# The last layer's token mixer as one block with an order per engine, and an expert ring of eight places

## What is computed

```
proj = hn @ w_in
u_pool, m_q, m_k, m_v, m_o, m_i, m_f, a_q, a_k, a_v = split(proj)
y_pool  = pool_mixer(u_pool, pool_w, pool_scale)      # window means 2, 4, 8, 16 less the value, times a 64x64 matrix
y_mlstm = mlstm_mixer(m_q, m_k, m_v, m_o, m_i, m_f)   # conv of 5 taps and silu on q, k; chunks of 128; both directions; 4 heads of 64
y_attn  = attn_mixer(a_q, a_k, a_v)                   # 8 query heads on 2 key heads of 64, head rmsnorm, rope, softmax
x = x + concatenate([y_pool, y_mlstm, y_attn]) @ w_out
x = x + mem_cross_attn(rmsnorm(x), mem)
x = x + ec_moe(rmsnorm(x))                            # 16 experts, each takes its 32 best tokens: gate-up 1024x4096, down 2048x1024
```

## Time and profile before

| | us |
|---|---|
| median of 3 runs | 4523.65 |
| lowest, highest | 4521.7, 4831.31 |
| profiled execution, its own time | 4513.02 |
| its span, first to last instruction | 4511.1 |

### The profile page before, as it was taken

One profiled execution on the slowest core, in us unless ns is written; L12 is line 12 of the kernel. 1 busy time (PEld: TensorE's weight loads), 2 busy tenths in 40 slices (PEclk: granted clock), 3 DMA queues, 4 the chain that ended last, 5 costly groups with the idle time before them and its releaser, 6 DMA issues. The chain is left out here.

```text
span 4511.1 us, 58281 instructions
## 1 busy us (share of the span) xinstructions
PE 3640.2 (81%) x19637; PEld 2637.3 (58%) x19637; DVE 2232.9 (49%) x4378; ACT 1565.4 (35%) x2639; POOL 168.1 (4%) x344
## 2 busy tenths in 40 slices
PE   7958987958699999998885599998367767767776
PEld 5638965547588888886555589997236322222223
DVE  5535643999566666665358778884442100000001
ACT  4424432138344444442241666663122111111111
POOL 0015600000000000000000000000000000000000
PEclk8979988979899999999897899999669788788888
DMA  4320023407654444553111599993212599999996
GB/s 181 112 78 13 14 94 121 168 26 221 223 186 176 168 174 179 186 186 131 55 47 38 150 371 312 311 310 123 112 38 85 211 428 427 428 428 427 427 428 272
DMA packets 331811, 909.62 MB, mean 202 GB/s; under 512 B 46592, under 2 KB 167168, under 8 KB 306176
## 3 DMA queue, kind: packets, MB, share of 16 engines
q1 hardware_dynamic: 331648, 907.42, 53.4%
HBM read 854.38 MB, written 52.95 MB: 201 GB/s over the span
## 5 line engine op out<-in xcount | busy, mean ns | idle before, releaser
L2002 PE MATMUL pd<-h_parts,u_parts 128*128 128x512 f32 x2048 | 472.5, 391 | 38.1 <-DVE u_parts L2088 38.1
L2015 PE MATMUL po<-act_parts,v_parts 128*128 128x512 f32 x2048 | 483.5, 393 | 9.4 <-DVE v_parts L2093 2.8
L2002 PEld LDWEIGHTS pd<-h_parts,u_parts 128*128 128x128 f32 x2048 | 386.3, 189 | 119.1 <-DVE u_parts L2088 38.3
L2015 PEld LDWEIGHTS po<-act_parts,v_parts 128*128 128x128 f32 x2048 | 383.7, 189 | 104.2 <-DVE v_parts L2093 21.2
L3126 PE MATMUL pb<-moe_ring,moe_xs 128*32 128x512 f32 x2048 | 330.7, 757 | 140.0 <-DMA moe_ring<-in_moe_gu 125.1
L3177 DVE TENSOR_TENSOR moe_hidden<-moe_silu,pg 128x512 f32<-128x512 f32 x16 | 11.0, 688 | 661.6 <-PE pg L3115 576.2
L2206 PE MATMUL pd<-h_parts,u_parts 128*128 128x256 f32 x2048 | 268.1, 284 | 38.5 <-DVE u_parts L2285 38.5
L2206 PEld LDWEIGHTS pd<-h_parts,u_parts 128*128 128x128 f32 x2048 | 264.6, 192 | 50.1 <-DVE u_parts L2285 39.1
L2216 PE MATMUL po<-v_parts,act_parts 128*128 128x512 f32 x1024 | 260.0, 398 | 0.9 <-DVE act_parts L2301 0.9
L395 PE MATMUL ps<-h_terms,w_terms 128*128 128x512 f32 x960 | 224.8, 397 | 37.6 <-DVE w_terms L408 37.6
L2052 ACT ACTIVATE acts<-pd 128x512 f32<-128x512 f32 x128 | 76.5, 598 | 492.7 <-PE pd L2002 492.7
(11 more groups left out here) (486 smaller groups left out, 5839.0 us busy)
## 6 DMA issues: line engine op xcount, KB each, us to landing
moe_ring<-in_moe_gu SPq DMA_DIRECT2D x128, 2048.0 KB, 27.0
u_stream<-in_peer_u SPq DMA_DIRECT2D x256, 512.0 KB, 6.1
v_stream<-in_peer_v SPq DMA_DIRECT2D x256, 512.0 KB, 4.3
moe_ring<-in_moe_down SPq DMA_DIRECT2D x64, 2048.0 KB, 26.3
ada_ring<-in_ada_w SPq DMA_DIRECT2D x20, 2048.0 KB, 14.2
g_stream<-peer_gates SPq DMA_DIRECT2D x128, 256.0 KB, 5.5
peer_gates<-gate_stage_even SPq DMA_DIRECT2D x3, 8192.0 KB, 30.3
peer_gates<-gate_stage_odd SPq DMA_DIRECT2D x3, 8192.0 KB, 30.3
```

The source lines that it names most:

```text
L2002: m = pe.matmul(pd[:, j, 0:T], us[:, j, w, c], h[:, w, c], start=(c + w == 0), stop=(c == DC - 1 and w == 1))
L2015: m = pe.matmul(po[:, (c + b) % 4, 0:T], vs[:, j, w, (c + b) * P:(c + b) * P + P], aparts[:, 4 * half + j, w], start=(j + w == 0), stop=(j ...
```

## The change

The stages of the mixer from its linear to its attention become one block, `mixer_block`, with a written order for each engine; the order of the projection's chunks changes with it (query and key of the mLSTM first, then pooling, attention key, attention queries, output gate; the host reorders the weights to match). Chunks and some small products share two PSUM banks in the order `MIX_ORDER`: an entry waits until the entry two before it has been taken. Pooling runs on GpSimd. The row broadcasts are matmuls with a column broadcast to 128 as weights. The exps run per head with the maximum as bias. The query norm is applied to the rows of scores (`rq`) with the scaling; only the key is normalised before rope. The finish of the mLSTM stands between the attention's units on VectorE (`finish`), with a root on ScalarE after unit 11 and its transposes on TensorE after unit 13. Attention has two places for scores, one bank for transposes (`tb`) and one for outputs (`ob`).

The expert ring has eight places in place of six, none of them filled in the mixer; all eight are asked for in the norm ahead of routing, behind the router's weights. The experts' loops on SyncE take turns of 24 tiles.

```
+MIX_ORDER = ("c0 c1 c2 c3 c4 c5 c6 c7 k_sum c8 c9 k_swap c10 swap0 q_sum c11 swap1 swap2 c12 swap3 pool0 pool1").split()
+            @block.sync
+                for g in range(2, 4):
+                    sp.wait_ge(made.h, made.at((g - 1) * 4))
+                    w_in.fetch(sp, g, g % 2)
+                w_out.begin(sp)
+            @block.gpsimd
+                link(pool.memset(sums[:], 0.0))
+                pool.wait_ge(psum_free.h, psum_free.at(MIX_POOL + 2))
+                link(pool.tensor_copy(sums[:, 0, :, mid], pT[:, MIX_POOL:MIX_POOL + 2]))
+                pool.wait_ge(arrived.h, arrived.at(tables.n))
+                for n, (back, on) in enumerate(((1, 0), (1, 1), (2, 2), (4, 4))):
...
+                    link(pool.tensor_tensor(sums[:, n + 1, :, a:b], sums[:, n, :, a - back:b - back], sums[:, n, :, a + on:b + on], ALU.add))
+                for g in range(4):
...
+                    link(pool.tensor_tensor(d[half, c], sums[half, g + 1, c, mid], rc[half, c], ALU.mult))
+                    link(pool.tensor_tensor(d[half, c], d[half, c], pT[half, MIX_POOL + c], ALU.subtract))
+            @block.tensor
...
+                for ch in range(4):
+                    chunk(ch)
+                tokens(0)
+                tokens(1)
+                k_turn()
+                chunk(4)
+                chunk(5)
+                cumulate()
+                chunk(6)
+                for q in (0, 2, 1, 3):
+                    rows(q)
+                products(1)
+                chunk(7)
+                products(0)
+                k_sum()
+                chunk(8)
+                chunk(9)
+                for q in (2, 3, 0, 1):
+                    weights_turn(q)
+                swap("k_swap", MIX_AK)
+                chunk(10)
+                numerators()
+                states()
+                swap("swap0", MIX_AQ)
+                q_sums()
+                chunk(11)
+                carried()
+                swap("swap1", MIX_AQ + 1)
+                swap("swap2", MIX_AQ + 2)
+                chunk(12)
+                swap("swap3", MIX_AQ + 3)
+                pool_products()
+                for x in range(N + 3):
...
+                    n = x - 2
+                    if 0 <= n < N:
+                        pe.wait_ge(normed.h, normed.at(n + 1))
+                        if n:
+                            pe.wait_ge(copied.h, copied.at(n))
...
+                    if x == Y_TURN:
+                        y_turn()
+            @block.scalar
...
+                padded(0)
+                padded(1)
+                squash(0)
+                padded(2)
+                squash(1)
+                padded(3)
+                squash(2)
+                tokens(0)
+                squash(3).then_inc(sca.h, 1)
+                tokens(1)
...
+                act.wait_ge(vec.h, vec.at["absolute"])
+                link(act.activation(tmp[:], tmp[:], ACT.Exp, scale=-1.0))
+                act.activation(tmp[:], tmp[:], ACT.Ln, bias=1.0).then_inc(sca.h, 1)
+                plain(4)
+                plain(5)
+                gained(MIX_AK, ak2[:], "k_norm_g")
+                gained(MIX_AQ, aq2[:, 0], "q_norm_g")
+                act.wait_ge(vec.h, vec.at["even"])
+                exps((0, 2)).then_inc(sca.h, 1)
+                act.wait_ge(vec.h, vec.at["args"])
+                exps((1, 3))
+                act.activation(arg[:], arg[:], ACT.Exp).then_inc(sca.h, 1)
+                gained(MIX_AQ + 1, aq2[:, 1], "q_norm_g")
...
+            @block.vector
...
+                dve.wait_ge(sca.h, sca.at["exp_odd"])
+                for dr in (1, 0):
+                    dve.wait_ge(ten.h, ten.at[f"qk{dr}"])
+                    for e in range(2):
+                        for q in (2 * dr, 2 * dr + 1):
...
+                            m = dve.scalar_tensor_tensor(out=dm[:, q, e:MH:2], in0=qk, scalar=0.125, in1=dm[:, q, e:MH:2], op0=ALU.mult, op1=ALU.mult)
+                    m.then_inc(vec.h, 1)
...
+                dve.wait_ge(sca.h, sca.at["k_root"])
+                link(dve.reciprocal(ak2[:], ak2[:]))
+                dve.wait_ge(psum_free.h, psum_free.at(MIX_AK + 1))
+                dve.tensor_tensor(ak, ak, ak2[:], ALU.mult).then_inc(vec.h, 1)
...
+                        dve.tensor_scalar(s[:, x % RING], place(len(MIX_ORDER) + x), rq[:, qt, 2 * j + e:2 * j + e + 1], AD ** -0.5, ALU.mult, ALU.mult).then_inc(scaled.h, 1)
...
-        pool_mixer(k, pT[:, 0:2, :], catT, pool_w, params, later)
-        mixer_conv(k, pT[:, 2:6, :], params, (experts,))
-        mlstm_mixer(k, pT[:, 2:6, :], pT[:, 6:8, :], tok[:, :, 0:256].rearrange("p t (h n) -> p t h n", n=AD), tok[:, :, 256:272], catT, params, consts)
...
+            mixer_block(k, hT, pT, tok, catT, pool_w, params, consts, later, tables, w_in, w_tok, w_out)
...
+FIRST_SLOTS = 0
-W_RING = 6
+W_RING = 8
+TURN_TILES = 2 * TILES
...
-        self.ring = k.sb(ctx, "moe_ring", [W_RING, 8 * BANK])
+        self.ring = [k.sb(ctx, "moe_ring", [8 * BANK]) for n in range(FIRST_SLOTS)]
...
+    def grow(self, k, ctx):
+        self.ring += [k.sb(ctx, "moe_ring_more", [8 * BANK]) for n in range(FIRST_SLOTS, W_RING)]
...
+        def begin(self, sp):
+            for n in range(FIRST_SLOTS, W_RING):
+                self.stream.fetch(sp, 0, n, n)
...
+                with sp.Fori(1, NE // 2) as turn:
+                    for m in range(TURN_TILES):
+                        sp.wait_ge(used.h, turn * TURN_TILES + used.at(m - W_RING + 1))
+                        stream.fetch(sp, turn * 2 + m // TILES, m % TILES, m)
...
+            norm_T(k, xT[:, :, CTX:TALL], DC, SEQ, hT, C("one"), {(0, SEQ): PARAMS(params, "norm_ffn_g")}, begin=(w_router, more))
```

More of the change, by code:

```diff
@@ L1476, in gdn_layer @@
             residual_linear(k, parts, 8, TALL, xT, w_out, mod, 2, split=True)
[L1479 to L1513, removed]
 def residual_linear(k, hT, kc, T, xT, stream, mod=None, part=None, x0=0, split=False):
@@ L2559, in swa_layer, with __init__, end @@
         residual_linear(k, oT, DC, SEQ, xT, w_out, mod, 2, x0=CTX)
+class Steps:
+    def __init__(self, sig, names):
+        names = names.split()
+        self.sig, self.h, self.n = sig, sig.h, len(names)
+        self.at = {x: sig.at(i + 1) for i, x in enumerate(names)}
+    def end(self):
+        self.sig.done(self.n)
 MH = 4
-def pool_mixer(k, uT, catT, pw, params, later):
+MIX_CHUNKS = 13
+MIX_QK, MIX_POOL, MIX_AK, MIX_AQ, MIX_O = 0, 4, 6, 7, 11
+MIX_ORDER = ("c0 c1 c2 c3 c4 c5 c6 c7 k_sum c8 c9 k_swap c10 swap0 q_sum c11 swap1 swap2 c12 swap3 pool0 pool1").split()
@@ L2593, in _ @@
-                link.end()
-        with nc.Block() as block:
-            @block.tensor
-            def _(pe):
-                for c in range(2):
-                    for h in range(2):
-                        half = slice(64 * h, 64 * h + 64)
-                        m = pe.matmul(ps[half, c, 0:SEQ], pw[half, c], d[half, c], start=True, stop=True)
-                    m.then_inc(made.h, 1)
-            @block.vector
-            def _(dve):
-                for c in range(2):
-                    dve.wait_ge(made.h, made.at(c + 1))
-                    dve.tensor_scalar(catT[:, c], ps[:, c, 0:SEQ], PARAMS(params, "pool_scale")[:, c:c + 1], None, ALU.mult)
@@ new lines, in masked, with maxima @@
+                def masked(q):
+                    row = M[:, q].rearrange("p (a n) -> p a n", n=P)
+                    add = mask[:, q // 2].rearrange("p (a n) -> p a n", a=1).broadcast_to([P, MH, P])
+                    return dve.tensor_tensor(dm[:, q], row, add, ALU.add)
+                def maxima(q):
+                    return dve.tensor_reduce(mx[:, q], dm[:, q], AX.X, ALU.max)
+                for q in (0, 2):
+                    dve.wait_ge(ten.h, ten.at[f"rows{q}"])
+                    dve.tensor_reduce(row_mx[:, q // 2], M[:, q].rearrange("p (a n) -> p a n", n=P), AX.X, ALU.max)
+                    link(masked(q))
+                    m = maxima(q)
@@ new lines, in _, with mixer_layer @@
+                link.end()
+    loaded[0].done(DMA_DONE * 2)
+    loaded[1].done(DMA_DONE * 2)
+    tok_loaded.done(DMA_DONE)
+    made.done(MIX_CHUNKS)
+    psum_free.done(MIX_CHUNKS)
+    achain.done(1)
+    pooled.done(POOL_STEPS)
+    arrived.done(tables.n)
+    for x in (vec, sca, ten):
+        x.end()
+    for x in (scored, scaled, maxed, neg, expd, inv, normed, turned, copied, outed, taken):
+        x.done(N)
+Y_ROOT, Y_TURN = 11, 13
+def mixer_layer(k, xT, pool_w, params, consts, later, tables, W):
+    C = lambda name: CONSTS(consts, name)
@@ L3182, in moe_experts @@
     for s in slot:
-        s.done(DMA_DONE * ROUNDS * NE)
+        s.done(DMA_DONE * ROUNDS * (NE // 4))
     used.done(TILES * NE)
@@ L3315, in host_rest @@
     aq = aq.reshape(D, 8, AD)[:, ATT_ORDER].reshape(D, 512)
-    out["mix_w_in"] = np.concatenate([pool, mq, mk, mo, aq, ak, mv, mi, mf, av], 1)
+    out["mix_w_in"] = np.concatenate([mq, mk, pool, ak, aq, mo, mv, mi, mf, av], 1)
```

756 lines of the change are left out of this document (460 added, 296 removed).

## The result

| | us |
|---|---|
| kernel before, median of 4 runs beside it | 4522.67 |
| changed kernel, median of 4 runs (4394.73 to 4399.96) | 4398.3 |
| ratio, 95% interval | 0.9733 (0.9722 to 0.9745) |
| profiled execution of the changed kernel, its span | 4398.47, 4396.5 |

One of the four executions of before (4831.31) was a slow one; it stands in the median above and not in the ratio.

The account below looks back on a forecast made before the run. Before attention no single engine was taken to bound (they take turns), in attention TensorE at half clock, in the experts DMA. Savings 116.8 + 1.2 + 9.9 = 127.9 from the median 4523.65 gave 4396 us, range 4370 to 4422.

Parts of the forecast that it names:

- The block: Last layer's mixer up to attention: TensorE's order 81.5, waits 0.9 and 0.8, clock 5, so 88.2 against 205.0, 116.8 saved.
- The key swap waits 0.9: In the block, TensorE's key swap waits 0.9 us for a chain of exps held behind chunk 7's evacuation on ScalarE.
- The clock term of 5: In the block, 5 us added, between 0 and 10.4, for TensorE's clock lost after transposes and narrow matmuls.
- Without it the cost would be 12: Pooling on GpSimd takes 12 us, done at 48 and wanted at 80; without that cover it would cost 12.
- Attention: Last layer's attention: 44 us taken, between ends at full and half clock, against 45.2 before; 1.2 saved.
- half-clock end: Attention at half clock: TensorE bounds units at 2.8 us, y's turn and part of the table loads add 2; 47 us.
- cold case: Rival, chance 0.15: half clock in attention (47), 10.4 for the block's clock, 6 for cold small matmuls; 4410 us.
- full-clock end: Attention at full clock: units near 2.0 us, with head and tail, a root and two table loads; 39 to 40 us.
- The ring: Expert weights: eight 2 MB tiles resident at the start in place of six, two fewer at 4.96 us; 9.9 saved.
- Full clock throughout: Rival, chance 0.19: block and attention at full clock take 122.7 us; 4386 by the median, 4376 by the profiled time.
- turns: Rival, chance 0.06: a queue holds an instruction behind a wait and nothing overlaps from chunk 5 on; 4441 us.
- slower stream: Rival, chance 0.02: the expert stream loses rate with eight separate buffers; at 360 GB/s the kernel takes 4556 us.

Follow-up runs that it names:

- e7: Changed kernel with ScalarE taking the even gates' exponents ahead of the first query chunk's gain; 4391.44 us, block 80.8.
- e11: Changed kernel with four reciprocals of 256 columns, into a tile nobody reads, put back on VectorE ahead of the query rotations; 4393.6 us, block 86.4.
- e10: Changed kernel with the pooling's 13 steps on VectorE, behind the gates' arguments, instead of GpSimd; 4394.97 us, block 85.7.
- e3: Changed kernel with attention scores summed over 128 rows, the other head's 64 key rows being zeros; 4386.38 us, attention 43.1.
- e9: Changed kernel with the mean's root after the last exponent and y's scaling, turn and gate after the units; 4393.39 us, attention 49.0.
- e8: Changed kernel with turned weights and outputs each in two PSUM banks in turn from the sixth unit on; 4393.12 us, attention 49.5.
- e4: Changed kernel with scores over 128 rows and products with v over 128 columns; 4382.66 us, ratio to before 0.9707, attention 42.6.
- e12: Changed kernel with 128-row scores, 128-column v, two banks in turn, exponents first and the late root together; 4376.16 us, ratio to before 0.9686, attention 37.3.
- e2: Changed kernel with the products with v over both heads' 128 columns, only the wanted half copied out; 4390.33 us, attention 49.7.
- e1: Changed kernel with the attention's transposes written as full matmuls against the identity; 4407.76 us, attention 59.0.
- e5: Changed kernel with the expert ring back at six places; 4408.72 us, ratio to before 0.9764.
- e6: Kernel before, its mixer functions kept, with only the ring of eight places filled in norm and routing; 4503.06 us, ratio 0.9973.

## Why the prediction was right, and where it was off

**The block, 116.8 predicted, 119.9 measured: right.** (Part of the finish's time went over into the attention, as said above.) The sum of TensorE's order, 81.5, can be read against e7, which has no long wait and no clock lost: 79.5 busy. The weights' 16 transposes took 2.2 where the prediction had 3.65 (its row came from a stage at a mean clock of 0.57), the row broadcasts 3.7 for 3.65, an exp 0.30 for 0.22, a weighing 0.34 for 0.49. "The key swap waits 0.9": it waited 1.8. The chain named for it, exponents behind chunk 7's evacuation, is the one that e7 removed. The pool evacuation's wait was 0.94 for 0.8. The clock term of 5 was too high: 1.7 in the executions in which the clock was lost, 0 in others, and it was lost in another place, behind the wait at the swap and not behind transposes and narrow matmuls. (The low clock at the block's start was in the sum: the 6.52 us of the first chunk gives 16.87 for four, and it took 16.86.) The queries' reciprocals, "VectorE 7 us less", had no price in the sum, and e11 gives them at most 1.3.

**GpSimd: right, but the 12 us are not what the move is worth.** Pooling took 12.0 us (3155.85 to 3167.82) and was done 47.6 us in, as predicted (12 and 48), 35 us ahead of its use. "Without it the cost would be 12" is GpSimd's own time with nothing beside it, and no run takes the cover away. Left on VectorE, the pooling costs 0.5 to 2.2 (e10).

**Attention, 44 predicted, 51.8 measured: the step that failed.** The prediction took the middle between full clock (39 to 40) and half clock (47), reasoning that the stage now begins behind dense chunks. It did begin at 1.00, and lost it in 4 us; how it starts doesn't decide, its own 64-row scores do (e3 against the change, one edit). The evidence stood in the earlier trace rows: 0.50 with TensorE busy 3.00 of 3.00 can't be a matter of a cold start. The half-clock end was itself 4.8 short. Two terms that it took as nearly free are that: root and table loads 2.8 (e9), single banks at the end 2.3 (e8). "Part of the table loads add 2", with the turn of y, held them for half hidden; a queue that feeds every unit has no slack for 2.8 us. Taken away, they lead back from 51.8 to 46.7, near the 47 of the cold case; that is a subtraction, no run has both at half clock. The full-clock end was low as well. It counted the root and its loads and came to 39 to 40 (its terms, 33, 2.6 and 2.8, add up to 38.4); e3 and e4, which have the root and the single banks, took 43.1 and 42.6, with the clock down to 0.92 and 0.88 on average by dips at the start and behind the root's wait. Units with the finish between them took 2.2 to 2.3 us, not 2.0. Without the root and the single banks it is 37.3 (e12).

The Trainium skill, "TensorE: Matmul & The Clock Gate" (What's actually happening), has the gate set by how busy TensorE was. The windows of e2 and e3 disagree as far as busy means records on TensorE: 4.00 of 4 us at 0.50 with 64-row scores, 2.46 of 4 at 1.00 with 128-row ones. The prediction also weighed its part on PE-mode transpose against the change; e1 took every transpose out of the attention and the clock stayed at 0.53 on average, so here that rule doesn't explain the loss.

**Behind the attention, 4.5 not in the sum.** The residual linear starts with matmuls at half clock (two in 1.19 above) and took 42.1 for 39.4. In e3, e4, e8 and e12 it took 39.3 or 39.4. What decides is whether the clock is back before the linear. In the kernel before and in e8, whose attentions ran at 0.52 and 0.55, the turns and products behind the last score follow each other without a wait, and the clock rises there; in the change they have waits (0.69 and 0.45 above) and it stays low. Windows of the last products, in the kernel before, in e8_two_banks and in the change:
```profile
3364.00:3368.00 4.00, 3.58 (x18) 2.11 (x16) 0.67 (x3) 2.44 (x9) 0.00 (x0) 0.72 0.01 4
```
```profile
3252.00:3256.00 4.00, 3.15 (x18) 2.18 (x17) 0.00 (x0) 1.20 (x4) 0.00 (x0) 0.95 0.00 0
```
```profile
3252.00:3256.00 4.00, 3.55 (x15) 2.41 (x14) 0.00 (x0) 1.31 (x4) 0.00 (x0) 0.50 0.00 0
```
In the first two the clock came back while products of 64 columns and transposes still ran and only the 64-row scores had ended, which fits e1 to e3. So the single banks cost twice, 2.3 in the attention and 1.4 to 2.9 behind it: the kernels that have them beside 64-row scores took 40.8 to 42.2 in the residual linear. The memory layer took 88.5 to 91.9; the difference lies in its first two linears (15.44 and 14.05 us before, 16.24 and 14.05 in the change, 17.06 and 15.74 in e8), and what sets it isn't shown.

**The ring, 9.9 predicted: right.** 912.3 us for 184 tiles, as worked out; e5 and e6 show it alone, 9.5 by e5's trace, 10.4 and 12 by medians. The stage as a whole gave 7.8, since the end behind the last tile took 2.1 us more (39.4 for 37.3, with its first small products at the lower clock, 3.62 us for 1.90). In e5 they took 1.90. Norm and routing, the prediction's 64, were not slowed by the DMA beside them (0.59 share in place of 0.01): 63.5 us before and 63.4 now, from the norm's first matmul to the experts' first. The 0 of the prediction stands.

**Rivals.** Full clock throughout (4386) falls to the 0.50 of the change's attention; the cold case (4410) was right that the attention runs at half clock, though not about its length (47 for 51.8), and wrong about the block; turns (4441) and a slower stream (4556) show nowhere: TensorE is busy 96% of the block, the stream at its old 4.96 per tile.

## What to carry to other kernels

When stages with one busy engine each become one block with an order per engine, add up the busiest engine's order; here that sum and two short waits gave the length within 4%. Then look at every engine's queue for something long in front of the next small step that another engine needs: a table load between two exponents, or exponents behind an evacuation, costs its full length in a loop with no slack, and a wait on TensorE may cost its length again in clock (1.7 us behind a wait of 1.8, in four of nine traces). And if a loop runs at half clock while TensorE is never idle, change the shape of its operands, not its order: rows of zeros that cost no time (a 64-row and a 128-row matmul took the same 1.22 at half clock) brought 9 us in a stage of 52.

## What the runs showed of the hardware that I had not expected

- Zeros in the unused 64 rows of the scores gave full clock, but for two dips, to a loop that was at 0.50 for 40 us (e3), with less TensorE time, not more. Wide products without it did not (e2).
- A wait of 1.8 us on TensorE after 40 dense us was followed by half clock (chunk 10 in 4.8 us) in four executions and not in five others with the same wait. The four are those in which the clock had risen later at the block's start (16.8 us for the first four chunks, 15.5 to 16.4 in the five).
- VectorE's steps of 8 to 16 columns took 0.69 to 1.08 us beside GpSimd's pooling and 0.17 without it (e10), but not all of them: L3014, between two stretched ones, took 0.16. The Trainium skill, "SBUF — State Buffer" (Who interferes with whom), describes a port pair that the two engines share under an exclusive lock; the rows agree with such a lock: L3013 and L3015 end within 0.03 us of the GpSimd steps of 0.72 that began just ahead of them (3164.69 and 3165.49).
